# The first step behind two norms, for one half of the tokens and then for the other

## What is computed

```python
h = rms_norm(x, g_attn_pre[l]) * (1.0 + scale_a[:, None]) + shift_a[:, None]
proj = h @ w_in[l]
...
mixed = jnp.concatenate([diff_out, dsa_out], axis=-1) @ w_o[l]
x = x + gate_a[:, None] * rms_norm(mixed, g_attn_post[l])
h = rms_norm(x, g_ffn_pre[l]) * (1.0 + scale_f[:, None]) + shift_f[:, None]
ff = (jax.nn.silu(h @ w_gate[l]) * (h @ w_up[l])) @ w_down[l]
```

## Time and profile before

| | us |
|---|---|
| median of 3 runs | 2508.11 |
| lowest and highest | 2507.94, 2508.81 |
| the profiled execution | 2507.55 |
| its span | 2505.8 |
| PE busy | 2471.1 (99%) |
| DVE busy | 1779.0 (71%) |
| ACT busy | 1228.2 (49%) |

### The profile page before, as it was taken

How to read it: one execution, slowest core, us unless ns; L and a number is a source line. 1 busy time by engine, 2 the same in 40 slices (tenths; PEclk the granted TensorE clock), 3 DMA queues, 4 the chain that set the end, 5 groups by cost and what they waited for, 6 DMA issues and landing times.

```text
span 2505.8 us, 33149 instructions
## 1 busy us (share of the span) xinstructions
PE 2471.1 (99%) x13297; PEld 2105.5 (84%) x13297; DVE 1779.0 (71%) x2425; ACT 1228.2 (49%) x1801; POOL 0.2 (0%) x4
## 2 busy tenths in 40 slices
PE   8999999999999999999999999999999999999998
PEld 7888877888888888888887899877788888888887
DVE  6557667677788888788888768776766556665555
ACT  6456456444544444443444444565545444443553
POOL 0000000000000000000000000000000000000000
PEclk9999999999999999999999999999999999999999
DMA  7555544888778879879778555455677667667554
...
DMA packets 324775, 573.32 MB, mean 229 GB/s; under 512 B 28659, under 2 KB 124301, under 8 KB 323725
## 3 DMA queue, kind: packets, MB, share of 16 engines
...
...
## 4 chain that ended last, share of the span: by engine, by line
PE 96%; DVE 2%; ACT 1%; issue 1%; DMA 0%; ACTq 0%; DVEq 0%; SPq 0%
PE ps L488 28%; PE ps L517 15%; PE ps L519 14%; PE ps L518 14%; PE ps L492 14%; PE ps L1010 2%; PE ps L1011 2%; PE ps L1012 2%; ACT wh L1090 1%; DVE wl L1792 0%; DVE ts L1916 0%; DMA xin<-x 0%; PE ps L939 0%; PE ps L757 0%; PE ps L895 0%
## 5 line engine op out<-in xcount | busy, mean ns | idle before, releaser
L1792 DVE TENSOR_TENSOR wl<-raw,wh 128x1024 fp32r<-128x1024 f32 x856 | 1041.0, 1224 | 688.7 <-ACT wh L1090 686.5
L1090 ACT ACTIVATE wh<-raw 128x1024 fp32r<-128x1024 f32 x856 | 899.4, 1058 | 1070.8 <-PE ps L519 503.7
L488 PE MATMUL ps<-hs,wh 128*128 128x512 f32 (+1 forms) x3152 | 994.4, 397 | 0.9 <-DVE hs L1864 0.5
L492 PEld LDWEIGHTS ps<-hs,wl 128*128 128x128 f32 (+1 forms) x3152 | 592.9, 188 | 141.2
L492 PE MATMUL ps<-hs,wl 128*128 128x256 f32 (+1 forms) x3152 | 620.6, 278 | 0.0
L488 PEld LDWEIGHTS ps<-hs,wh 128*128 128x128 f32 (+1 forms) x3152 | 481.4, 189 | 3.0 <-issue 1.1
L517 PE MATMUL ps<-wh,ff 128*128 128x512 f32 x864 | 336.1, 389 | 0.0
L518 PE MATMUL ps<-wl,ff 128*128 128x512 f32 x864 | 336.1, 389 | 0.0
L519 PE MATMUL ps<-wh,ff 128*128 128x512 f32 x864 | 336.1, 389 | 0.0
L517 PE MATMUL ps<-wh,hs 128*128 128x512 f32 x640 | 256.7, 401 | 0.0
L519 PE MATMUL ps<-wh,hs 128*128 128x512 f32 x640 | 250.0, 391 | 0.0
...
## 6 DMA issues: line engine op xcount, KB each, us to landing
...
```

The costliest lines, as they stand in the source:

```text
L488: nc.tensor.matmul(ps[0:m, b, :], wh[:, slot, w0:w0 + m], rhs(n, k), start=k == 0, stop=False)
L492: mm = nc.tensor.matmul(ps[0:m, b, 0:T], wl[:, slot, w0:w0 + m], rhs(n, k)[:, 0:T], start=False, stop=k == 4 * panels - 1)
L1090: nc.scalar.activation(wh[:, h % WH_SLOTS, :], raw[:, slot, HALF * q:HALF * (q + 1)], ACT.Copy).then_inc(wh_ready, 1)
L1792: nc.vector.tensor_tensor(wl[:, h % WH_SLOTS, :], raw[:, slot, HALF * q:HALF * (q + 1)], wh[:, h % WH_SLOTS, :], ALU.subtract).then_inc(wl ...
```

## The change

`first_step` replaces `step` at both places. It walks halves 0 to 3 of the weights for tokens 0 to 127, then the same halves again for tokens 128 to 255, then goes on with `step` at half 4 for all tokens. Its matmuls with `wh` have 256 columns (128 rounded and 128 rest), those with `wl` 128. `half_used` counts a half only in the second walk. Pieces 0 to 3 are now made separately for each half of the tokens, with 128 columns an instruction (`rows_piece`); pieces 4 to 7 stay whole. Transposes go with them: the first two groups (of the first tokens) stand at place 1 three quarters through the last phase of the down projection, at place 2 behind it, the others between the halves of the first walk, those of pieces 4 to 7 in the second walk and behind half 4. DVE scales only quarters 0 and 1 of the rows; ACT scales quarters 2 and 3 (`rows_scaled`), behind its roundings. The order of DVE and ACT is rewritten; at place 2 the second norm of the first tokens now stands ahead of the x updates of the others.

```diff
+            def first_step(p, t, f, turns):
+                pe.wait_ge(tile_summed, 4 * t + 4)
+                for i in range(2):
+                    for h in range(4):
+                        slot = (2 * p + h) % WH_SLOTS
+                        pe.wait_ge(sem("hs_lo"), LO_BEFORE[f] + 8 * i + 2 * h + 2)
+                        if i == 0:
+                            pe.wait_ge(wl_ready, 2 * p + h + 9)
+                        for n, (c0, m) in enumerate(FULL):
+                            b = bank(t, n)
+                            for kk in range(2):
+                                k, w0 = 2 * h + kk, 512 * kk + c0
+                                nc.tensor.matmul(half_of(ps[0:m, b, :], i), wh[:, slot, w0:w0 + m],
+                                                 half_of(hs[:, k, :], i), start=k + i == 0, stop=False)
+                            for kk in range(2):
+                                k, w0 = 2 * h + kk, 512 * kk + c0
+                                mm = nc.tensor.matmul(ps[0:m, b, i * P:(i + 1) * P], wl[:, slot, w0:w0 + m],
+                                                      hs[:, k, i * P:(i + 1) * P], start=False, stop=False)
+                        if i:
+                            mm.then_inc(half_used, 1)
+                        turns(i, h)
+                step(p, 0, t, 0, FULL, from_hs, split=(sem("hs_lo"), LO_BEFORE[f] + 8), done=4,
+                     after={4: lambda: rows_turn(f, 7)})
...
+                        if i and h == last - 1 and early is not None:
+                            early()
...
+                mm.then_inc(sem("rows_turned"), 1)
+            def turns_between(f):
+                def turns(i, h):
+                    if (i, h) == (0, 1):
+                        rows_turn(f, 3, (0,))
+                    if (i, h) == (0, 2):
+                        rows_turn(f, 0, (1,))
+                        rows_turn(f, 1, (1,))
+                    if (i, h) == (0, 3):
+                        rows_turn(f, 2, (1,))
+                        rows_turn(f, 3, (1,))
+                    if i and h:
+                        rows_turn(f, 3 + h)
+                return turns
...
-                           split=(sem("ff_lo"), 16 * c) if d == 0 else None, apart=4 if (c, d) == (3, 3) else 0)
+                           split=(sem("ff_lo"), 16 * c) if d == 0 else None, apart=4 if (c, d) == (3, 3) else 0,
+                           early=(lambda: first_turns(0)) if (c, d) == (3, 3) else None)
             for c in range(4):
                 ffn_chunk(c)
-            rows_turns(0)
+            rows_turn(0, 2, (0,))
...
-            step(L7.panel, 0, L7.step, 0, FULL, from_hs, split=(sem("hs_lo"), ND * FILL_A),
-                 after={h: turn_after(0, 3 + h) for h in range(5)})
+            first_step(L7.panel, L7.step, 0, turns_between(0))
...
-            rows_turns(1)
+                       split=(sem("hs_lo"), ATT_BEFORE + 8) if s == 0 else None, apart=4 if s == 3 else 0)
+            first_turns(1)
+            rows_turn(1, 2, (0,))
...
+            def rows_scaled(f, q, r):
+                i, src, dst = ((R_A, x_rows, a_rows), (R_F, x_back, f_rows))[f]
+                c = slice(512 * q, 512 * q + 512)
+                if r == 0:
+                    act.wait_ge(sem("rows_normed"), 4 * f + 1)
+                else:
+                    act.wait_ge(sem("rows_normed"), 4 * f + 3)
+                nc.scalar.activation(dst[:, r, c], src[:, r, c], ACT.Copy, scale=row_root[i][:, r:r + 1]
+                                     ).then_inc(sem("rows_scaled"), 1)
...
+                            hs_high(0, 0, 0)
                             row_square(8 * R_A + 7, R_A, x_rows, 3, 1, across_summed, 40)
                             row_roots(R_A, 3, OTHERS)
-                            hs_high(0, 0)
-                            hs_high(0, 1)
-                            hs_high(0, 2)
+                            hs_high(0, 1, 0)
...
+            hs_high(0, 2, 0)
+            hs_high(0, 3, 0)
+            rows_scaled(0, 2, 0)
+            rows_scaled(0, 2, 1)
+            for j in range(4):
+                hs_high(0, j, 1)
+            rows_scaled(0, 3, 0)
+            rows_scaled(0, 3, 1)
...
+            row_roots(R_F, 5, FIRST)
             row_square(last + 11, R_MIXED, mix_rows, 3, 1, across_summed, 48)
-            row_roots(R_MIXED, 5, OTHERS)
+            row_roots(R_MIXED, 6, OTHERS)
             feed(2 * LF2.panel + 1, 0)
-            row_roots(R_F, 6, FIRST)
+            hs_high(1, 0, 0)
+            hs_high(1, 1, 0)
+            feed(2 * LF2.panel + 2, 0)
             for d in range(4):
                 row_square(last + 12 + d, R_F, x_back, d, 1, sem("row_updated"), d + 5)
+            hs_high(1, 2, 0)
             row_roots(R_F, 7, OTHERS)
-            hs_high(1, 0)
-            hs_high(1, 1)
-            feed(2 * LF2.panel + 2, 0)
-            hs_high(1, 2)
             feed(2 * LF2.panel + 3, 0)
+            hs_high(1, 3, 0)
+            rows_scaled(1, 2, 0)
+            rows_scaled(1, 2, 1)
+            for j in range(4):
+                hs_high(1, j, 1)
+            rows_scaled(1, 3, 0)
+            rows_scaled(1, 3, 1)
...
-                    if u[0] + u[1] == 0 and h < 5:
-                        hs_high(1, 3 + h)
+                    if u[0] + u[1] == 0 and h < 4:
+                        hs_high(1, 4 + h)
...
-            def rows_value(f, j):
-                _, _, _, gain, shift, fill = FILLS[f]
-                dve.wait_ge(sem("rows_turned"), 8 * f + j + 9)
+            def rows_value(f, j, i=None):
+                _, _, _, gain, shift, _ = FILLS[f]
+                turned = j + (4 if j >= 4 or i else 0)
+                dve.wait_ge(sem("rows_turned"), 8 + 12 * f + turned + 1)
                 for k in (2 * j, 2 * j + 1):
                     if k >= 4:
-                        dve.wait_ge(sem("hs_lo"), ND * fill + k - 3)
-                    nc.vector.tensor_scalar(ts[:, k % 4, :], ps[:, 4 * f + j % 4, (k % 2) * T:(k % 2 + 1) * T],
+                        dve.wait_ge(sem("hs_lo"), LO_BEFORE[f] + piece(k - 4, 1 if i is None else i) + 1)
+                    nc.vector.tensor_scalar(ts[:, k % 4, columns(i)], ps[:, 4 * f + j % 4, columns(i, k % 2 * T) if i is not None
+                                                                         else slice(k % 2 * T, k % 2 * T + T)],
                                             gain[:, k:k + 1], shift[:, k:k + 1], ALU.mult, ALU.add
                                             ).then_inc(sem("hs_value"), 1)
...
-            def rows_fill(f, next_half, late=None):
-                fill = FILLS[f][5]
-                rows_normed(f, 0, 1)
-                rows_value(f, 0)
-                rows_normed(f, 1, 1)
-                hs_low(fill, 0)
-                rows_value(f, 1)
-                if late is not None:
-                    feed(late, 0)
-                hs_low(fill, 1)
-                rows_value(f, 2)
-                feed(next_half, 0)
-                hs_low(fill, 2)
-                rows_normed(f, 2, 1)
-                rows_normed(f, 3, 1)
-                feed(next_half + 1, 0)
+            def rows_piece(f, j, i=None):
+                rows_value(f, j, i)
+                hs_low(f, j, i)
...
-                if h < 5:
-                    rows_value(f, 3 + h)
-                    hs_low(FILLS[f][5], 3 + h)
+                if h < 4:
+                    rows_piece(f, 4 + h)
...
             row_add(37, last, 2, x_rows, x_rows, 3, 0)
             rows_reduce(R_A, 8 * R_A + 7, FIRST)
             rows_invert(R_A, 2, FIRST)
-            for q in range(4):
-                rows_normed(0, q, 0)
+            rows_normed(0, 0, 0)
+            rows_normed(0, 1, 0)
             feed(2 * last, 0)
+            rows_piece(0, 0, 0)
             row_add(37, last, 2, x_rows, x_rows, 3, 1)
             feed(2 * last + 1, 0)
             rows_reduce(R_A, 8 * R_A + 8, OTHERS)
+            rows_piece(0, 1, 0)
+            feed(2 * last + 2, 0)
             rows_invert(R_A, 3, OTHERS)
-            rows_fill(0, 2 * last + 2)
+            rows_piece(0, 2, 0)
+            rows_normed(0, 0, 1)
+            rows_normed(0, 1, 1)
+            feed(2 * last + 3, 0)
+            rows_piece(0, 3, 0)
+            for j in range(4):
+                rows_piece(0, j, 1)
...
             row_add(47, LF2.panel, 6, mix_rows, mix_rows, 3, 1)
+            rows_reduce(R_F, last + 11, FIRST)
             feed(2 * LF2.panel, 0)
+            rows_invert(R_F, 5, FIRST)
+            rows_normed(1, 0, 0)
+            rows_normed(1, 1, 0)
             rows_reduce(R_MIXED, last + 12, OTHERS)
             mixed_gain(3, 1, last + 12)
-            rows_invert(R_MIXED, 5, OTHERS)
-            rows_reduce(R_F, last + 11, FIRST)
+            rows_piece(1, 0, 0)
+            rows_invert(R_MIXED, 6, OTHERS)
+            feed(2 * LF2.panel + 1, 0)
+            rows_piece(1, 1, 0)
             mixed_into_x(1)
-            rows_invert(R_F, 6, FIRST)
```

(13 more changed lines are left out.)

67 lines of the change are left out of this document (39 added, 28 removed).

## The result

The changed kernel takes 2513.40 us (median of 13 runs), the kernel before 2507.97 on the same chip: ratio 1.0022, 95% interval 1.0014 to 1.003. That is 5.4 us slower and 1.1 above the 2512.3 forecast, inside the range of 2509.3 to 2516.6. 0.22% is just past the border of 0.2% that the forecast drew between no change (chance 0.57) and slower (0.38), and the interval reaches to both sides of it. The span of the profiled execution is 2511.6, 5.8 more than before.

A forecast was written before the change was run, and what follows sets the result against it. The prediction took the step's end as set by when DVE writes piece 4's value, plus three turns and 1.95 us. +0.9 and +3.3 make +4.2: span 2505.8 to 2510.0, median 2512.3, range 2509.3 to 2516.6.

The forecast's parts named there:

- place 1: Fill of the first step behind the attention norm; PE starts 5.4 us earlier, yet the end comes 0.9 later.
- place 2: Fill of the first step behind the feed-forward norm; PE starts 5.7 us earlier, yet the end comes 3.3 later.
- three turns: From piece 4 to piece 7, DVE and ACT alternate in a loop of 3.57 us a turn, slower than PE.
- The waits ahead of halves 6 and 7: Sign of being right: PE's waits on DVE in halves 6 and 7 grow to 0.7 us each.
- narrow piece: A piece for 128 tokens on DVE, values and subtractions with waits for ACT: 1.30 us, bounds 1.1 and 1.8.
- PE's slack at place 1: PE's own work would reach half 7 at 1397.1, before DVE allows it at 1398.35: 1.3 us.
- ACT's scaling: ACT scaling 512 columns, taken as 0.53 us; two of them, 1.06, stand ahead of wh 4.
- the new wait for wh 3: At place 2 ACT makes wh 3 only behind the other tokens' root, so DVE waits 1.4 us.
- B: Slower rival: narrow operations pay their full fixed part, pieces about 1.6 us, 2.4 more at each place, 2517.1; chance 0.24.
- C: Slower rival: PE's clock falls in the stop-and-go of place 1, +2.4 us, 2514.7; chance 0.08.
- D: No-loss rival: pieces at the lower bound 1.1 gain 1.6 us at each place, 2509.1; chance 0.11.
- E: Faster rival: the early start is kept, by 5 us at place 1, giving 2502; chance 0.05.

The follow-up runs named there:

- e1: Against the changed kernel, ACT makes the weights of half 4 (wh 4) ahead of its last two row scalings at both places; 2511.29 us.
- e3: Against the changed kernel, PE leaves out the wl matmuls in its eight walks at both places, so the result lacks that part; 2512.61 us.
- e7: Against the changed kernel, PE fills its gaps at place 2 with unread identity matmuls short enough to fit; 2512.68 us.
- e8: Against the changed kernel, two halves walked twice instead of four, pieces 2 to 7 whole, e2's ACT order, scalings moved, x_back updates ahead of piece 1; 2505.02 us.
- e11: Against the kernel walking only one half twice, PE fills its gaps at place 2 with 3, 2 and 3 identity matmuls; 2501.65 us.
- e2: Against e1, ACT makes wh of the next half ahead of a piece's conversions, at both places; 2511.09 us.

## Why the forecast was right in kind, and what was mis-sized

**What bounds.** That DVE's value of piece 4 and three turns set the end is shown by e1 (1.25 earlier, PE's waits gone) and e3 (no PE work, no gain). In e3 PE still waited 2.94 us. The turn is 3.57 in the changed kernel too: (1396.89 - 1386.19)/3. From the last value to half 7 it is 1.96 (1398.85 - 1396.89), forecast 1.95. PE's first walks start at 1368.66 and 1756.89 on the old scale, forecast 1368.6 and 1756.8. The waits ahead of halves 6 and 7 were to grow to 0.7 each; they are 0.45 and 0.51 at place 1 and 0.51 at place 2, there ahead of half 7 only.

**Prices.** A narrow piece takes 1.31 (1380.46 - 1379.15), forecast 1.30. A walk takes 1.84, forecast 1.87. PE's slack at place 1 was 1.3 in the forecast; half 7 by PE's own work would be at 1388.56 + 3.22 + 5.6 = 1397.4, which is 1.4 before 1398.85 (in e1, where nothing holds it up, it is at 1397.59).

**Place 1: +1.28, forecast +0.9.** The value of piece 4 starts at 1386.19 - 0.14 = 1386.05, forecast 1385.7. The term that was mis-sized is ACT's scaling: I took 0.53 between two rows of conversions, and it is 0.62 from start to start and 0.71 long, so 1.23 for two instead of 1.06. The other 0.2 is a slip in where ACT stands when DVE is through. DVE's own list was right: it ends at 1383.08 - 0.14 = 1382.94 (the last pair of subtractions starts at 1382.55, and a pair takes 0.53), forecast 1366.9 + 16.1 = 1383.0. Within it two errors cancel: the two pieces that ACT serves late take 1.61 and 1.63, 0.6 more than 1.31 each where I had 0.4, and the wait of 0.2 for the add did not come. But ACT's first scaling starts 0.34 before that end (1382.74), where the forecast had ACT free at 1382.4, 0.6 before it. ACT's two DMAs were issued while it computed and cost nothing.

**Place 2: +4.41, forecast +3.3.** wl 3 starts at 1767.10 - 1.44 = 1765.7, and the new wait for wh 3 is 1.31, forecast 1.4. Up to there all is as said. The value of piece 4 is at 1780.10 - 1.44 = 1778.66 instead of 1777.5. From wl 3 on it is 1.3 us more than forecast (13.0 against 1777.5 - 1765.8 = 11.7), since wl 3 itself came 0.1 early. Most of it, 0.81 of waiting and 0.9 with what DVE needs to start again, is a wait that the forecast doesn't have: DVE's value of the third piece of the second tokens at 1774.37, for transposes that stand behind PE's walk of half 3. I had written that walks at the low clock "fall into waits for DVE". For walks 0 and 1 that holds. For the walk of half 3 it doesn't: the clock fell a second time, the walk took 3.0 us (1770.68 to the transposes at 1773.68), and behind it stood something DVE wanted. This wait is the term that the forecast had at nothing; e3 and e7, where it is gone, are 0.9 us shorter there. 0.2 is the scaling again, and 0.1 the piece that ACT serves late (1.63, forecast 1.5); the rest is rounding.

**What luck did.** The span grew by 5.8 us and not 4.2, a miss of 1.6. Of that, 0.14 lies ahead of the places, and 0.5 doesn't show in the median: the forecast added 2.31 to the span (1.75 and 0.56, both read off the kernel before), and in the changed kernel the median is only 2513.40 - 2511.6 = 1.8 above it. So the 1.1 between 2512.3 and 2513.4 makes the sum look better than it was.

**Rivals.** B, the full fixed part for narrow operations, needed pieces of 1.6; they take 1.31. What the Trainium skill says in "VectorE: DVE Perf Modes" (section "The TRN2 errata — SBUF-src ops pay a fixed extra latency per instruction"), that many small tiles pay the fixed part each, is a rule for operations that read SBUF (the values here read PSUM), and points the right way all the same: a wide piece takes 1.82 in e8 (1379.07 - 1377.25), two narrow ones 2.62, so cutting four pieces costs DVE 3.2 us at each place. That much of the fixed part is paid, and e8 to e11 spare a part of it. They also spare PE part of the doubled walks (1.8 us in e8) and take e2's order on ACT, and no run separates these. C, the clock at place 1, didn't happen in the changed kernel (it did in e3, whose walks are half as long); what the clock took, it took at place 2. D (2509.1) and E (2502) needed a DVE that is through earlier.
